# A fused decoder layer: the weight sums of the down projection made in another order on GpSimd

## The reference

```
x = x + rms_norm(mix, mix_norm_post)
h = rms_norm(x, ffn_norm_pre)
u = causal_dwconv(h @ w_up, ffn_conv)              # width 3
gate, up = split(u, 2)
ffn = (silu(gate) * up) @ w_down                   # 1024 x 2816 times 2816 x 1024
x = x + rms_norm(ffn, ffn_norm_post)
x = x + rms_norm((p @ w_ple) * sigmoid(x @ w_ple_gate), ple_norm_post)
```

## Time and profile before

| | before |
|---|---|
| median of three runs | 1472.25 us |
| the profiled execution | 1471.73 us |
| its span, first to last instruction | 1470.0 us |
| PE busy | 1425.7 us, 97% |
| DVE busy | 1041.9 us, 71% |
| ACT busy | 702.8 us, 48% |
| POOL busy | 353.3 us, 24% |
| mean granted clock of PE | 0.993 |
| down projection, first unit to last | 1129.8 to 1343 us |

### The profile page before, as it was taken

How to read it: one execution, slowest core, us unless ns; L and a number is a source line. 1 busy time by engine, 2 the same in 40 slices (tenths; PEclk the granted TensorE clock), 3 DMA queues, 4 the chain that set the end, 5 groups by cost and what they waited for, 6 DMA issues and landing times.

```text
span 1470.0 us, 19630 instructions
## 1 busy us (share of the span) xinstructions
PE 1425.7 (97%) x7167; PEld 1200.7 (82%) x7167; DVE 1041.9 (71%) x1467; ACT 702.8 (48%) x1297; POOL 353.3 (24%) x314
## 2 busy tenths in 40 slices
PE   6999999999989999999999999999999999999996
PEld 5777888878879999888888888787788888888885
DVE  6666545552027888357897999999999785577566
ACT  6432457422226788347674343334435444454434
POOL 3000001100018777010013333333330144410010
PEclk9999999999998999999999999999999999999998
DMA  8553423545622332544442334334326765424232
GB/s 222 78 105 44 43 66 122 151 108 112 153 79 72 109 102 80 185 145 158 150 129 80 105 110 144 115 115 158 105 97 225 249 193 192 143 79 130 86 101 101
DMA packets 156318, 181.52 MB, mean 123 GB/s; under 512 B 21240, under 2 KB 96190, under 8 KB 156222
## 3 DMA queue, kind: packets, MB, share of 16 engines
q1 hardware_dynamic: 155968, 180.16, 42.6%
q10 hardware_dynamic: 254, 0.10, 0.0%
HBM read 130.95 MB, written 49.28 MB: 123 GB/s over the span
## 4 chain that ended last, share of the span: by engine, by line
PE 84%; DVE 10%; issue 2%; ACT 2%; DMA 1%; POOL 0%; SPq 0%; DVEq 0%; ACTq 0%; POOLq 0%
PE psum L2254 7%; PE psum L2255 7%; PE psum L2256 7%; PE psum L563 5%; PE psum L564 5%; PE psum L565 5%; PE psum L1202 5%; PE psum L2193 4%; PE psum L2195 4%; PE psum L2194 4%; PE psum L2166 4%; PE psum L2167 4%; PE psum L2168 4%; PE psum L1256 3%; PE psum L618 3%; PE psum L620 3%
## 5 line engine op out<-in xcount | busy, mean ns | idle before, releaser
L148 DVE TENSOR_TENSOR w_wlo<-w_raw,w_whi 128x1024 fp32r<-128x1024 f32 x70 | 93.8, 1340 | 253.5 <-ACT w_whi L142 253.4
L2254 PE MATMUL psum<-m_hi,w_whi 128*128 128x512 f32 x416 | 163.0, 392 | 7.1 <-DVE w_wlo L1821 6.2
L2255 PE MATMUL psum<-m_lo,w_whi 128*128 128x512 f32 x416 | 161.9, 389 | 0.0
L2256 PE MATMUL psum<-m_hi,w_wlo 128*128 128x512 f32 x416 | 161.9, 389 | 0.0
L142 ACT ACTIVATE w_whi<-w_raw 128x1024 fp32r<-128x1024 f32 x70 | 74.0, 1057 | 183.5 <-PE psum L2168 85.5
L563 PE MATMUL psum<-h_hi,w_whi 128*128 128x512 f32 x320 | 126.7, 396 | 2.8 <-DVE h_lo L834 2.8
L564 PE MATMUL psum<-h_lo,w_whi 128*128 128x512 f32 x320 | 125.3, 392 | 0.0
L565 PE MATMUL psum<-h_hi,w_wlo 128*128 128x512 f32 x320 | 125.2, 391 | 0.0
L2193 PE MATMUL psum<-w_whi,g_slot 128*128 128x512 f32 x308 | 120.1, 390 | 0.6 <-DVE w_wlo L2968 0.6
L2194 PE MATMUL psum<-w_wlo,g_slot 128*128 128x512 f32 x308 | 119.9, 389 | 0.0
L2195 PE MATMUL psum<-w_whi,g_slot 128*128 128x512 f32 x308 | 119.8, 389 | 0.0
(11 more groups left out here) (377 smaller groups left out, 3577.7 us busy)
## 6 DMA issues: line engine op xcount, KB each, us to landing
w_raw<-in_w_up SPq DMA_DIRECT2D x39, 512.0 KB, 3.9
w_raw<-in_w_in SPq DMA_DIRECT2D x36, 512.0 KB, 6.5
s_rows<-formed_sums SPq DMA_DIRECT2D x11, 1024.0 KB, 4.1
w_raw<-s_rows SPq DMA_DIRECT2D x44, 256.0 KB, 2.7
g_rows<-long_g SPq DMA_DIRECT2D x18, 512.0 KB, 2.7
w_raw<-g_rows SPq DMA_DIRECT2D x33, 256.0 KB, 3.9
w_raw<-in_w_out SPq DMA_DIRECT2D x16, 512.0 KB, 4.4
mixed_home<-in_w_down SPq DMA_DIRECT2D x32, 256.0 KB, 4.1
```

Source lines behind the costliest of these rows:

```text
L2254: pe.matmul(out, wh[:, part], hi(kt), start=(start and kt == 0), stop=False)
L2255: pe.matmul(out, wh[:, part], lo(kt), start=False, stop=False)
L2256: ins = pe.matmul(out, wl[:, part], hi(kt), start=False, stop=(stop and kt == KT // 2 - 1))
```

## The change

`pool_down` makes T3[i] directly behind T2[i], in one loop, and T4 last. The `left` waits for a later piece are replaced by waits for the piece that reads the tile's old content: T1[i] waits for piece i, T2[i] for piece 22 + i, T4[i] for piece 11 + i, T3[i] for none. `made_count` follows the new order. And `home_gap` is 16 columns wide in place of 24, so all that is allocated behind it lies 32 bytes lower.

```diff
-        gap = s("home_gap", [P, 24])
+        gap = s("home_gap", [P, 16])
...
     def made_count(self, m, i):
 
-        return {2: 0, 4: 1, 6: 2, 5: 3}[m] * self.KH + i + 1
+        n = self.KH
+        return {2: i + 1, 4: n + 2 * i + 1, 5: n + 2 * i + 2, 6: 3 * n + i + 1}[m]
...
-        made, left = self.s["down_made"], lambda u: self.units.ready(pool, self.piece(u))
+        made, split = self.s["down_made"], lambda m, i: self.units.ready(pool, self.piece(m * self.KH + i))
         home = lambda which: self.w_home(which, i)
         for i in range(self.KH):
             self.w_landed(pool, self.B12, i)
-            left(self.KH + self.AHEAD + i)
+            split(0, i)
             pool.tensor_tensor(home(self.B11), home(self.B12), home(self.B11), ALU.subtract).then_inc(made, 1)
         for i in range(self.KH):
             self.w_landed(pool, self.B22, i)
             pool.wait_ge(made, self.made_count(2, i))
-            left(2 * self.KH + self.AHEAD + i)
+            split(2, i)
             pool.tensor_tensor(home(self.B11), home(self.B11), home(self.B22), ALU.subtract).then_inc(made, 1)
+            pool.tensor_tensor(home(self.B12), home(self.B22), home(self.B12), ALU.subtract).then_inc(made, 1)
         for i in range(self.KH):
             pool.wait_ge(made, self.made_count(4, i))
-            left(3 * self.KH + self.AHEAD + i)
+            split(1, i)
             pool.tensor_tensor(home(self.B21), home(self.B21), home(self.B11), ALU.add).then_inc(made, 1)
-        for i in range(self.KH):
-            left(4 * self.KH + self.AHEAD + i)
-            pool.tensor_tensor(home(self.B12), home(self.B22), home(self.B12), ALU.subtract).then_inc(made, 1)
```

## The result

With the change the kernel takes 1482.37 us (median of four runs, 1480.94 to 1483.81) against 1471.99 before: 10.4 us more, a ratio of 1.0072 with a 95% interval of 1.0054 to 1.0089. I had said 1478.4, and at most 1481.5. The direction and the mechanism that I described are in the trace; a second cost that I had put at zero is there too.

A forecast was written before the change was run, and what follows sets the result against it. PE, busy for 97% of the span, bounds the kernel; 33 dense POOL ops taking turns with DVE make it 6.1 us late. 1471.7 + 6.1 = 1477.9, plus 0.5 to the median gives 1478.4 us; range 1475.0 to 1481.5.

The forecast's parts named there:

- (6): Allocation: with home_gap at 16 columns, tiles behind it lie 32 bytes lower; zero cost, 0.5 us allowed either way.
- (1): Down projection, T1: its waits for a later piece go, but the load of B12[i] still paces it; no change.
- (2): Down projection, T2: its loads still pace it, the removed wait was not the last one; no gain.
- (5): Semaphore counts: ACT gets the same tiles, all ready before it asks; zero.
- (3): Down projection: T3 moves right behind T2[i], waiting only for the engine; in the dense POOL block that costs 6.1 us.
- (4): Down projection: T4 becomes eleven POOL ops in a row, its waits long met; in the block that costs 6.1 us.
- Part on PSUM adds: Down projection: four block adds behind pieces 26 to 29 run in POOL's time, costing nothing; 2.2 us if they competed.
- PE waits ... some 0.7 us each: Down projection, 1217 to 1248 us: PE waits for DVE's w_wlo nine or ten times, 6.1 us more in all.
- Rival A: Down projection: POOL yields to DVE, one op per unit, so PE never waits; 1472.3 us, chance 0.11.
- B: Down projection: PE's waits also halve its granted clock for one stretch, 2.6 us more; 1480.9 us, chance 0.05.
- C: Down projection: a POOL and DVE turn takes the full recorded 1.98 us; 1487.1 us, chance 0.02.
- D: Faster: one 0.6 us wait, or part of the pair stage's 6.2 us through new addresses, is won; 1471.0 us, chance 0.04.

## Why the prediction was wrong

The step that failed is number (6), "What is allocated behind it lies 32 bytes lower ... Zero; I allow 0.5 us either way". Alone it measured 4.04 us in the down projection, where on top of the new order it added 2.66 (8.71 less 6.05), and in both cases 0.6 more where `p_hi` and `p_lo` are loaded (from the start of that part to the last matmuls the trace of after grew from 8.9 to 9.55 us behind that of before). Its rows showed how DVE reads and how loads land. PE, which sets the time here, reads `g_slot` too, and I did not ask what a matmul does with another distance between its operands. No row of before could have priced it: all its large matmuls stand at 226 or 227 ns, and the tiles that they read start, by the allocations, at the same remainder by 256. That should have widened the range, not closed it: a cost without a row was set to zero by rows of another engine. At the 7 ns measured since, all 7167 matmuls would make 50 us, and those that read tiles behind the gap 5: a bound of that kind was what the range lacked.

Point by point:
- Parts (1), (2), (5), T1, T2 and ACT's counts: right. With the order alone the trace has no new wait outside the block.
- Parts (3) and (4), the block of 33 POOL ops and its sum: right in mechanism and size. 1.70 us per turn, on record from 1193.88 to 1249.69 (said: 1192.9 to about 1249); 6.05 us in the stage with the order alone for 6.1 said; nine waits in the block for "nine or ten".
- Part on PSUM adds, and the rule of the Trainium skill (SBUF — State Buffer, section SBUF: two separate sides) on ops with two SBUF inputs: the four adds run inside POOL ops, as said; the order-only stage leaves no room for 2.2 us more.
- Said too sharply: "PE waits ... some 0.7 us each" in the view of waits. Lost are 0.68 us a unit with the order alone and 0.60 with both edits; on record as idle are 0.33 to 0.39.
- The range: its ends, 1475.9 and 1481.5, leave out the 0.5 us from the profiled execution to the median that the forecast itself has. With it they are 1476.3 and 1482.0, and 1482.37 is outside these too.
- Rival A, POOL yields: out. B, the clock: out, PEclk is 1.00 in the block. C, 1.98 us per turn: out. D named the addresses, but as a gain, and put PE's side at nothing.

The forecast missed by 4 us in 1482. In the traces 3.3 us of that come from the edit of one number (2.66 in the stage and 0.6 behind it); the rest is as small as the differences between executions of one kernel.

## What to carry to other kernels

Two engines that take turns, as POOL and DVE do here, fit as long as the one that is not critical is paced; count its ops per unit of the critical engine before letting it run ahead, for "as early as possible" cost 6 us here and gained nothing. An edit that moves tiles is an edit of the matmuls: keep the loaded tile (128 columns) and the streamed one (512 columns, float32) a multiple of 256 bytes apart, as far as these runs go, and look at the distance from matmul to matmul after every change of an allocation. A cost for which the trace has no row is unknown, and goes into the range with its bound.

## What the hardware showed that I had not expected

- A matmul of 128x128 by 512 float32 columns takes 226.7 ns from start to start where loaded and streamed tile lie a multiple of 256 bytes apart, and 228.9 to 234.3 at other multiples of 32 bytes. The price has a direction (64 bytes up 233.3, down 228.9) and is not there at 384 columns, for the three distances tried. Why is open.
- With the order changed, POOL and DVE took turns for 33 ops without one exception among the ops with both inputs in SBUF, though DVE was late and PE waited for it: 1.15 us for POOL, 0.55 for DVE.
- PE idled about a fifth of each unit in nine units and the granted clock stayed at 1.00.
